# The first slab's high passes for token tile 0 put between the two tiles' transposes of x, and each quarter's low weights taken last

## The reference

```python
def first_block(x, positions, ret_w_in, ...):
    h = x
    # layer 0
    q, k, v, g = jnp.split(x @ w_in, [H * dk, 2 * H * dk, 2 * H * dk + H * dv], axis=-1)
    v = v.reshape(B, S, H, dv).astype(jnp.float32)
```

## Time and profile before

| | us |
|---|---|
| median of 3 runs | 2145.84 (2145.38 to 2146.86) |
| the profiled execution, its own time | 2145.01 |
| its span, first to last instruction | 2143.0 |
| TensorE busy | 2055.5 (96%) |
| VectorE busy | 1328.3 (62%) |
| ScalarE busy | 921.0 (43%) |

### The profile page before, as it was taken

How to read it: one execution, slowest core, us unless ns; L and a number is a source line. 1 busy time by engine, 2 the same in 40 slices (tenths; PEclk the granted TensorE clock), 3 DMA queues, 4 the chain that set the end, 5 groups by cost and what they waited for, 6 DMA issues and landing times.

```text
span 2143.0 us, 28893 instructions
## 1 busy us (share of the span) xinstructions
PE 2055.5 (96%) x12296; PEld 1790.3 (84%) x12296; DVE 1328.3 (62%) x1300; ACT 921.0 (43%) x862; POOL 74.6 (3%) x49
## 2 busy tenths in 40 slices
PE   8999999998999879999999999989998999999998
PEld 7988888797887758887988888879987887998997
DVE  6765766788666547567656666665444456765444
ACT  5444433385333443333345433344344445554333
POOL 0000000100001000001000000010002000001000
PEclk9999999999999999999999999999999999999999
DMA  8443655445543414454535455525546454343542
GB/s 320 158 167 148 216 196 192 138 166 203 205 175 141 160 57 176 181 196 158 207 127 196 165 185 195 192 89 191 201 176 194 147 151 153 123 158 129 195 177 98
DMA packets 32373, 364.34 MB, mean 170 GB/s; under 512 B 3677, under 2 KB 3938, under 8 KB 10130
## 3 DMA queue, kind: packets, MB, share of 16 engines
q1 hardware_dynamic: 28146, 347.49, 44.1%
q0 software_dynamic: 4128, 15.39, 3.0%
HBM read 361.77 MB, written 1.10 MB: 169 GB/s over the span
## 4 chain that ended last, share of the span: by engine, by line
PE 83%; DVE 9%; ACT 5%; DMA 1%; issue 1%; SPq 0%; DVEq 0%; ACTq 0%
PE acc L884 26%; PE bank L832 9%; PE bank L834 9%; PE bank L833 9%; PE bank L1374 8%; PE bank L1376 4%; PE bank L871 3%; PE bank L873 3%; PE bank L872 3%; DVE h L2320 2%; ACT w_hi L1677 1%; DVE w_lo L2237 1%; DMA raw<-slabs_in 1%; PE bank L1513 1%; PE bank L1549 1%
## 5 line engine op out<-in xcount | busy, mean ns | idle before, releaser
L832 PE MATMUL bank<-ht_both,w_hi 128*128 128x256 f32 x1568 | 441.2, 281 | 0.1
L834 PE MATMUL bank<-ht_both,w_lo 128*128 128x256 f32 x1568 | 438.7, 280 | 0.0
L833 PE MATMUL bank<-ht_both,w_hi 128*128 128x256 f32 x1568 | 438.2, 279 | 0.0
L2237 DVE TENSOR_TENSOR w_lo<-raw,w_hi 128x4096 fp32r<-128x4096 f32 (+4 forms) x83 | 310.2, 3737 | 120.8 <-ACT w_hi L1677 120.7
L1665 ACT ACTIVATE w_hi<-raw 128x2048 fp32r<-128x2048 f32 x166 | 309.3, 1910 | 142.7 <-PE bank L834 138.8
L1677 ACT ACTIVATE w_hi<-raw 128x4096 fp32r<-128x4096 f32 (+4 forms) x91 | 283.5, 3115 | 182.1 <-PE bank L1376 156.7
L832 PEld LDWEIGHTS bank<-ht_both,w_hi 128*128 128x128 f32 x1568 | 295.2, 188 | 4.1 <-issue 3.0
L833 PEld LDWEIGHTS bank<-ht_both,w_hi 128*128 128x128 f32 x1568 | 295.2, 188 | 1.5 <-issue 0.5
L834 PEld LDWEIGHTS bank<-ht_both,w_lo 128*128 128x128 f32 x1568 | 295.5, 188 | 0.0
L2232 DVE TENSOR_TENSOR w_lo<-raw,w_hi 128x2048 fp32r<-128x2048 f32 x102 | 229.2, 2288 | 104.3 <-ACT w_hi L1665 104.2
L1374 PE MATMUL bank<-ht_both,w_hi 128*128 128x512 f32 x768 | 269.1, 393 | 0.0
(11 more groups left out here) (389 smaller groups left out, 3259.4 us busy)
## 6 DMA issues: line engine op xcount, KB each, us to landing
raw<-slabs_in SPq DMA_DIRECT2D x147, 2048.0 KB, 7.7
raw<-slabs_in SPq DMA_DIRECT2D x23, 1024.0 KB, 6.7
raw<-slabs_in SPq DMA_DIRECT2D x12, 512.0 KB, 10.9
g_tab<-gains_in POOLq DMA_DIRECT2D x11, 512.0 KB, 4.4
a_bias<-bias_rows POOLq DMA_DIRECT2D x8, 576.0 KB, 7.5
b_tab<-gains_in POOLq DMA_DIRECT2D x8, 512.0 KB, 5.2
raw<-slabs_in SPq DMA_DIRECT2D x2, 1152.0 KB, 5.7
raw<-slabs_in SPq DMA_DIRECT2D x1, 1280.0 KB, 5.6
```

The source lines that it names most:

```text
L832: nc.tensor.matmul(o, whi, xhi, start=first, stop=False)
L833: nc.tensor.matmul(o, whi, xlo, start=False, stop=False)
L834: return nc.tensor.matmul(o, wlo, xhi, start=False, stop=last)
L2237: nc.vector.tensor_tensor(w_lo[ring][:, 0:w], raw[ring][:, 0:w], w_hi[slot][:, 0:w].bitcast(F32), ALU.subtract).then_inc(lo_ready, 1)
```

## The change

`first_values` is cut into passes. A new `first_pass(t, q, high)` does, for one tile and one quarter, either the two passes per k that need only high weights (`ht_hi` and `ht_lo` with `w_hi`) or the one that needs low weights. A new `first_quarter` does the high passes of quarter 0 for token tile 0 (four passes), behind a wait for that quarter's high weights; it is called between the transposes of tile 0 and the wait for tile 1 of x. `first_values` then waits for each quarter's high weights, does the high passes of both tiles (of tile 1 alone in quarter 0), waits for the low weights, and does the low passes of both tiles. The number of passes and transposes is the same. Nothing is changed on the other engines' lists or in the queues.

```diff
--- before.py
+++ after.py
@@ -1024,27 +1024,40 @@
                         pe.wait_ge(*read("tr", tr, t, half))
                         ht_unseen.discard((tr, half, t))
 
+            def first_pass(t, q, high):
+
+                key, c = ("v", 0, 0, t), slice(t * P, (t + 1) * P)
+                for k in range(2 * q, 2 * q + 2):
+                    need_ht(k, [t])
+                    w = slice(k * 512, k * 512 + 512)
+                    if high:
+                        nc.tensor.matmul(psum(*key)[:, :], ht_hi[:, k, c], w_hi[0][:, w], start=k == 0, stop=False)
+                        nc.tensor.matmul(psum(*key)[:, :], ht_lo[:, k, c], w_hi[0][:, w], start=False, stop=False)
+                    else:
+                        m = nc.tensor.matmul(psum(*key)[:, :], ht_hi[:, k, c], w_lo[0][:, w], start=False,
+                                             stop=k == KD - 1)
+                if q == 3 and not high:
+                    m.then_inc(bank_full[ticket[key][0]], 1)
+
+            def first_quarter():
+
+                wait_free("v", 0, 0, 0)
+                pe.wait_ge(quarter_hi, 1)
+                first_pass(0, 0, True)
+
             def first_values():
 
+                wait_free("v", 0, 0, 1)
                 for q in range(4):
+                    pe.wait_ge(*((quarter_hi, q + 1) if q < 3 else (hi_ready, 1)))
+                    for t in range(1 if q == 0 else 0, TT):
+                        first_pass(t, q, True)
                     if q < 3:
                         pe.wait_ge(quarter_lo, q + 1)
                     else:
                         need(0)
                     for t in range(TT):
-                        key = ("v", 0, 0, t)
-                        if q == 0:
-                            wait_free(*key)
-                        c = slice(t * P, (t + 1) * P)
-                        for k in range(2 * q, 2 * q + 2):
-                            need_ht(k, [t])
-                            w = slice(k * 512, k * 512 + 512)
-                            nc.tensor.matmul(psum(*key)[:, :], ht_hi[:, k, c], w_hi[0][:, w], start=k == 0, stop=False)
-                            nc.tensor.matmul(psum(*key)[:, :], ht_hi[:, k, c], w_lo[0][:, w], start=False, stop=False)
-                            m = nc.tensor.matmul(psum(*key)[:, :], ht_lo[:, k, c], w_hi[0][:, w], start=False,
-                                                 stop=k == KD - 1)
-                        if q == 3:
-                            m.then_inc(bank_full[ticket[key][0]], 1)
+                        first_pass(t, q, False)
 
             def parameter_columns():
 
@@ -1631,9 +1644,11 @@
 
 
             pe.wait_ge(ident_loaded, 16)
-            for t in range(TT):
-                pe.wait_ge(x_loaded[t], 16)
-                transposes(None, t)
+            pe.wait_ge(x_loaded[0], 16)
+            transposes(None, 0)
+            first_quarter()
+            pe.wait_ge(x_loaded[1], 16)
+            transposes(None, 1)
             for layer in range(DEPTH):
                 (retention, lru, mla)[layer % 3](layer)
                 mlp(layer)
```

## The result

| | before | changed |
|---|---|---|
| median of 22 runs each | 2144.81 us (2141.34 to 2147.76) | 2148.42 us (2142.46 to 2150.32) |
| ratio of the runs | | 1.0016, 95% interval [1.0009, 1.0022] |
| the profiled execution: its time, its span | 2145.01, 2143.0 | 2149.52, 2147.4 |

The changed kernel is slower by 0.16%, some 3.4 us (0.0016 x 2145), within the 0.2% (4.3 us) that the prediction took as the bound, but clear of zero. Measured three more times with the experiments it gave 1.0011 [1.0002, 1.0019], 1.0015 [1.0006, 1.0024] and 1.0016 [1.0007, 1.0025].

The account below looks back on a forecast made before the run. TensorE, busy 2055.5 of 2143.0 us, was taken as the bound. With 0.49 won at the front and 0.8 lost behind the transposes, +0.3: 2145.01 becomes 2145.3, median 2146.1; range 2145.3 to 2146.9, with rival A and B 2144.9 to 2148.5.

Parts of the forecast that it names:

- rival A: Behind the new hole the clock's rise starts over at 13.6: total +2.1 to +2.7 us, time 2147.9 to 2148.5; chance 0.3.
- Step 1: TensorE's four early passes start at 9.27, once quarter 0's high weights are copied, filling 0.49 of the 2.83 us hole.
- Step 2: The four early passes run at the lower clock level: 4 x 0.425 = 1.70 us, from 9.27 to 10.97.
- Step 3: Tile 1's transposes start 1.24 us later, at about 11.0; TensorE then waits about 0.8 us for tile 1's parts.
- Step 4: The 44 remaining passes from 13.58: slab 1 begins +0.07, +0.22 or +0.6 us later by the clock's rise; +0.3 taken.
- Step 5: ACT and DVE work behind tile 1 shifts by up to 1.24 us, still covered; slab 1's low parts keep 1.2 us.
- B: Tile 1 lands 1.2 us or more later, so the early passes fill a wait: -0.9 us, time 2144.9; chance 0.04.
- C: Slower by over 0.2%: lower clock level through all 44 passes from 13.58, 8.4 us in all, time 2154.3; chance 0.03.
- D: Faster by over 0.2%, only if a later stage happens to run better; the whole hole is 2.83 us; chance 0.01.
- The low weights last: In the first passes nothing waits for low weights, so putting low passes last buys nothing by itself and can only cost.

Follow-up runs that it names:

- experiment 3: Kernel before with token tile 1 ahead of tile 0 in quarter 0, no early passes: 1.0010 [1.0001, 1.0020] of the kernel before, +2.1 us.
- experiment 6: Kernel before run again under a new name, nothing changed: 0.9998 [0.9989, 1.0007] of the kernel before.
- experiment 1: Changed kernel without the early quarter: both tiles transposed first, each quarter's high passes before its low ones; 1.0002 [0.9993, 1.0011], median 2145.16 against 2145.50 for the kernel before.
- 2, tile 0's low passes first: Changed kernel with tile 0's two low passes ahead of tile 1's high ones in quarter 0: 0.9996 [0.9987, 1.0005], median 2144.28 against 2145.50 for the kernel before.
- e7: Changed kernel with three filler matmuls (results unused) ahead of its early quarter: 1.0002 [0.9994, 1.0011] of the kernel before.
- e5: Kernel before plus three filler matmuls (results unused) between tile 0's transposes and the wait for tile 1 of x: 0.9996 [0.9987, 1.0004].
- e6: As e5, with one more filler matmul ahead of tile 0's transposes: 0.9996 [0.9988, 1.0005] of the kernel before.
- experiment 8: As experiment 1, plus two filler matmuls between tile 0's transposes and the wait for tile 1: 0.9995 [0.9986, 1.0004], median 2145.06 against 2146.30 for the kernel before.

## Why the prediction was right or wrong

The time, 2148.42, lies at the upper end of the range of 2144.9 to 2148.5, and "within 0.2%", held the likeliest, is what came. But the forecast was +0.3 and the ratio says 3.4, from 1.9 to 4.7 us; by size it is rival A (chance 0.3) that fits, not the forecast. The range's margin for chance came from three runs 1.5 us apart; the 22 runs lie 6.4 us apart, so that the time lies inside it is in part luck. Point by point:

- **Step 1 (passes from 9.27).** Read from one execution whose quarter 0 landed earliest. ACT's copy began at 9.16, 8.48, 9.00 and 8.68 in the four profiles, the passes at 10.31, 9.64, 10.16 and 9.83. The kernel before does not feel this landing; the changed one begins with it. So only 0.1 to 0.2 us of the wait were filled (the passes began that much before tile 1 landed), not 0.45. Tile 1's transposes began 1.6 to 1.8 us after its landing instead of 1.28, and its passes 4.2 to 4.3 instead of 3.86. This is what the three profiles lost whose clock was up in time.
- **Step 2 (1.70 for four passes)** held but for one small term: 11.48 - 9.64 = 1.84, since the spacing behind the restart is 0.56 and not 0.425. The sum had left that 0.14 out.
- **Step 3 (late transposes, a hole of 0.8)** held in place and cause: 0.65, 0.65, 0.65 and 1.04 us, on DVE's part of tile 1.
- **Step 4 is the one that failed, as a size.** It forecast +0.07 if the clock is up by the restart, +0.22 if it rises where it did before, +0.6 if a microsecond later. Net of the landing the start cost 0.5, 0.6, 0.6 and 2.2 us. In the three small ones the clock was up at the restart, where step 4 has +0.07; the rest is step 1's. The one of 2.2 is rival A as priced (2.1 to 2.7), and experiment 3's profile shows the same with the hole alone. The Trainium skill ("TensorE: Matmul & The Clock Gate", "A second HAM failure mode: psum-queue depth-cycling") speaks of short idle times between groups of matmuls with which the clock goes back and forth between its levels. No trace here shows that for this hole: after 0.65 us the lower level stood on in two (to 17.5 and about 18.5), and in three, with 0.65 or 1.04 us, it did not.
- **Step 5 (later work covered)** held: no TensorE wait in the start but the known ones; slab 1 did not wait for its low part. The shift was 1.7 to 2.3 us instead of 1.24, but slab 1 was as much later: its last low quarter was ready 1.3 us or more ahead of slab 1's start, where 1.2 had been forecast.
- **Rivals B, C, D** did not come. The first profile's other 1.3 us, the spacing of 0.118 from 50 to 83, was named by none; it is chance, and the kernel before has it too (experiment 6).
- **The low weights last** gained nothing, as the first part had it (experiment 1).

**What stays open.** The start explains 0.6 us in three profiles and 2.2 in one, about 1.0 on average; the times say 2.4 to 3.4. Behind slab 1's start the four profiles took 2120.7, 2118.2, 2120.6 and 2121.9, mean 2120.4, against 2119.2, 2118.9 and 2119.3 for the kernel before, its repeat and experiment 1. That would be the missing part, but the scatter within one kernel is as large. Two explanations offer themselves: the held clock is commoner in the timed runs than in four profiles, or a start shifted by half a microsecond changes the odds at later restarts, so that the lower level stands for longer there.

The timed runs speak against the second. Each has a mean granted clock, which tells how long the lower level stood; it leaves the start out, since it reads 1.00 there even while the spacings are those of the lower level (14 to 18 us in the first profile of the changed kernel). Over its runs the changed kernel has the same mean clock as the kernel before in three of its four measurements (0.9875, 0.9874 and 0.9874 against 0.9875 and 0.9876; 0.9869 in the fourth). And it is slower at equal clock. This comparison was made after the fact, with the clock given to three digits only; it takes the runs at 0.987, the commonest value, and of the kernel before those of the same rounds. The last column is the lead less 13.9, the mean of the kernel before's two profiles:

| version | runs, mean span | before: runs, mean span | difference | lead |
|---|---|---|---|---|
| changed (2nd, 3rd, 4th time) | 7, 7 and 10: 2146.1, 2146.6, 2147.0 | 22, 20, 20: 2144.2, 2144.5, 2144.5 | +1.9, +2.1, +2.4 | +0.6, +0.7, +0.7 (first profile +2.4) |
| 3, only the hole | 6: 2145.9 | 21: 2143.9 | +2.0 | +2.3 |
| 2, tile 0's low passes first | 6: 2143.9 | 21: 2143.9 | 0.0 | +0.6 |
| 1, order alone | 5: 2144.1 | 21: 2143.9 | +0.2 | +0.2 |
| 7, early quarter and fillers (e7) | 6: 2145.0 | 22: 2144.2 | +0.8 | +0.7 |
| 7, three fillers (e5) | 6: 2142.9 | 22: 2144.2 | -1.3 | -0.9 |
| 7, four fillers (e6) | 10: 2143.4 | 22: 2144.2 | -0.8 | -1.0 |
| 8, reordered, two fillers | 6: 2143.0 | 20: 2144.5 | -1.6 | -1.4 |
| 6, before again | 8: 2143.8 | 20: 2144.5 | -0.7 | -0.1 |

Each difference is uncertain by some 0.3 to 0.6 us. The other versions' large ones follow the lead of the profile, so what is won or lost at the start does come through to the end, and experiment 8's gain is probably real. The changed kernel is the exception: it loses some 2 us, which is near the outcome with the held clock, though three of its four profiles have the other. So the held clock is probably commoner in the timed runs than in the profiles. That is argued, not shown: no timed run shows the clock of its start, nor the pace of its 256-column passes, which could make part of the difference.

## What to carry to other kernels

Moving work into a wait pays only if what is behind the wait isn't itself the head of a chain over other engines: here four passes of 1.7 us filled 0.1 to 0.2 us of idle time and pushed back transposes whose result takes 2.5 us to come back. Before putting dependent work directly behind such a head, keep something independent (here tile 0's two low passes) for the time until it returns. A saving under a microsecond at the start of a long kernel is smaller than what the clock and the pace do at each later restart, so judge it by the stage's own rows over several profiles, or by runs of equal granted clock, and not by the total alone.

## What the hardware showed that was not expected

- The 256-column passes run wholly busy at granted clock 1.00 with a spacing of either 0.113 or 0.118 us from one restart to the next, the same instructions in different executions: 4%, 1.3 us over the 33 us from 50 to 83. One execution can have both: the kernel before has 0.118 before the restart near 50 and 0.113 behind it.
- The granted clock is shown as 1.00 from 9.76 to 13.80 where the spacings are those of the lower level, and in the first profile of the changed kernel still from 16 to 18 us, where six passes of 512 columns fall into the 2 us (ten in the kernel before).
- The same hole of 0.65 us at the start was followed by the lower level for over 3.5 us (changed kernel, first profile: 14.71 to 18.26) or not at all (its repeat). The Trainium skill ("TensorE: Matmul & The Clock Gate", "What's actually happening") says that how many matmuls of one kernel run slow differs from run to run; the four profiles agree (twelve slow passes of 512 columns in the first, four in each of the others).
- Quarter 0 and tile 1, issued at the same times in each execution, landed over a range of 0.9 to 1.0 us between executions (tile 1 at 9.5 to 10.4; ACT took up quarter 0 at 8.17 to 9.16).
